# A two-block transformer kernel: the output projection behind the attention loop cut into pieces by its last head, and three changes of order

## What is computed

```python
h = _rmsnorm(hres, norm_g[i, 0])
qkv = jnp.einsum('bld,de->ble', h, w_in)              # 8 heads, q and k of two parts of 64, v of 128
...
a = (p[:, :, 0] - lam * p[:, :, 1]).astype(v.dtype)   # p: softmax of each part with a distance bias
outs.append(jnp.einsum('bhqk,bkhe->bqhe', a, v[:, :qe]))
o = _rmsnorm(o, subln_g) * (1.0 - lam_init)           # per head
return jnp.einsum('ble,ed->bld', o.reshape(bsz, L, N_HEADS * V_DIM), w_out)
...
hres = hres + _rmsnorm(m, norm_g[i, 1])
```

## Time and profile before

| | us |
|---|---|
| median of 3 runs | 2134.41 (2129.05 to 2136.33) |
| the profiled execution, its own time | 2129.2 |
| its span, first to last instruction | 2127.4 |
| TensorE busy, by the page | 1990.0 (94%) |
| VectorE, ScalarE, GpSimd busy | 1056.7, 679.7, 175.9 |
| mean granted TensorE clock | 0.958 of full |

### The profile page before, as it was taken

The page is one execution under the profiler, slowest core; times in us unless marked ns, Lnnn a source line. Parts: engine busy times, 40 slices in busy tenths (PEclk is TensorE's granted clock), DMA queues, the critical chain, the costliest instruction groups (busy, mean ns, idle before and its releaser), DMA issues.

```text
span 2127.4 us, 27654 instructions
## 1 busy us (share of the span) xinstructions
PE 1990.0 (94%) x11486; PEld 1737.7 (82%) x11486; DVE 1056.7 (50%) x1480; ACT 679.7 (32%) x958; POOL 175.9 (8%) x127
## 2 busy tenths in 40 slices
PE   7898888999999988998979999999989989999996
PEld 5677676888888777888869999999989877888885
DVE  7573645543434567565644534333375555343344
ACT  4443433322222335333323413222332233233231
POOL 3000003100000202000003100000210031000002
PEclk9996899999999999999988999999999999999998
DMA  4120102222222321011102122222212222222221
GB/s 168 60 84 35 50 1 79 81 98 99 99 99 79 119 80 60 21 60 41 44 37 80 60 100 100 79 99 81 97 60 100 90 89 79 91 97 89 99 99 40
DMA packets 25907, 166.07 MB, mean 78 GB/s; under 512 B 3792, under 2 KB 4048, under 8 KB 6352
## 3 DMA queue, kind: packets, MB, share of 16 engines
q1 hardware_dynamic: 25808, 164.66, 21.8%
HBM read 162.55 MB, written 2.10 MB: 77 GB/s over the span
## 4 chain that ended last, share of the span: by engine, by line
PE 82%; DVE 11%; issue 4%; ACT 3%; DMA 0%; POOL 0%; SPq 0%; DVEq 0%; ACTq 0%; POOLq 0%
PE ps L306 23%; PE ps L307 23%; PE ps L308 23%; DVE z_lo L413 2%; DVE ps L462 2%; PE ps L1806 2%; DVE w_lo L288 1%; PE ps L1572 1%; DVE h L475 1%; ACT w_hi L277 1%; PE ps L1807 1%; PE ps L1808 1%; PE ps L1574 1%; PE ps L1573 1%; PE ps L1840 1%
## 5 line engine op out<-in xcount | busy, mean ns | idle before, releaser
L306 PE MATMUL ps<-z_hi,w_hi 128*128 128x512 f32 (+1 forms) x1744 | 612.9, 351 | 50.4 <-DVE z_lo L413 34.9
L307 PE MATMUL ps<-z_lo,w_hi 128*128 128x512 f32 (+1 forms) x1744 | 608.3, 349 | 0.0
L308 PE MATMUL ps<-z_hi,w_lo 128*128 128x512 f32 (+1 forms) x1744 | 607.0, 348 | 0.0
L288 DVE TENSOR_TENSOR w_lo<-w_raw,w_hi 128x2048 fp32r<-128x2048 f32 x152 | 348.2, 2291 | 161.6 <-ACT w_hi L277 161.5
L277 ACT ACTIVATE w_hi<-w_raw 128x2048 fp32r<-128x2048 f32 x152 | 289.8, 1906 | 424.3 <-PE ps L308 413.7
L306 PEld LDWEIGHTS ps<-z_hi,w_hi 128*128 128x128 f32 x1744 | 333.9, 191 | 105.0 <-issue 32.7
L306 PE MATMUL ps<-arena,w_hi 128*128 128x256 f32 (+1 forms) x1144 | 385.2, 337 | 5.5 <-DVE arena L1189 5.5
L307 PE MATMUL ps<-arena,w_hi 128*128 128x256 f32 (+1 forms) x1144 | 385.2, 337 | 0.0
L308 PE MATMUL ps<-arena,w_lo 128*128 128x256 f32 (+1 forms) x1144 | 384.6, 336 | 0.0
L308 PEld LDWEIGHTS ps<-z_hi,w_lo 128*128 128x128 f32 x1744 | 333.8, 191 | 44.3
L307 PEld LDWEIGHTS ps<-z_lo,w_hi 128*128 128x128 f32 x1744 | 334.0, 192 | 42.7 <-issue 0.7
(11 more groups left out here) (261 smaller groups left out, 1940.4 us busy)
## 6 DMA issues: line engine op xcount, KB each, us to landing
w_raw<-wstream SPq DMA_DIRECT2D x152, 1024.0 KB, 4.8
h<-xT SPq DMA_DIRECT2D x8, 256.0 KB, 7.1
out<-h SPq DMA_DIRECT2D x8, 256.0 KB, 2.0
rope_cs<-pT SPq DMA_DIRECT2D x1, 512.0 KB, 5.5
acc<-pos SPq DMA_DIRECT2D x1, 256.0 KB, 2.7
acc<-lam SPq DMA_DIRECT2D x1, 128.0 KB, 8.5
sm<-small SPq DMA_DIRECT2D x1, 86.0 KB, 2.5
h<-metaT SPq DMA_DIRECT2D x1, 64.0 KB, 8.8
```

Source lines behind the costliest of these rows:

```text
L288: dve.tensor_tensor(w_lo[:, slot, :], w_raw[:, slot, :], w_hi[:, slot, :].bitcast(f32), ALU.subtract).then_inc(wlo, 1)
L306: pe.matmul(dst, wh, zh, start=(k == 0), stop=False)
L307: pe.matmul(dst, wh, zl, start=False, stop=False)
L308: last = pe.matmul(dst, wl, zh, start=False, stop=(k == nk - 1))
```

## The change

1. The output projection's first six tiles are done in two parts. Part one (input heads 0 to 6, 42 pieces) fills the last head's gaps in the order `EARLY_ORDER`, is copied to `acc` by `out_part1`, and part two (input head 7, 6 pieces) is added by `add_acc_at` from other PSUM banks. Tiles 6 and 7 follow as one block. The weights lie in DRAM in the order of use.
2. The numbers of pieces between a head's steps change: [2] `d_pv(n-1, 1)` [1] `d_v(n)` [2] `d_t(u)` `d_s(u+2)` `o_columns` with [1] and [1] inside, [2] `o_spread` with [1] inside, `d_t(u+1)` `d_s(u+3)` [3] `d_t(u+2)` `d_s_last(u+4, 0)` [3] `d_s_last(u+4, 1)` [2] `d_pv(n, 0)` [1] `d_t(u+3)` [2] `d_s(u+5)` [3] `d_t(u+4)` `d_s(u+6)`. In the last head the three at `d_t(u+2)` are two, the one before `d_t(u+3)` is two, and the three before `d_t(u+4)` are four. Before `d_v(0)` there are three instead of two.
3. VectorE's second weight split of heads 0, 2, 4, 6 moves behind `d_mix(u+3)`.
4. In the first projection VectorE splits block b+1 before it takes the tiles of block b, for b = 3 to 6.

```diff
-MANY = {B_UQ: 4, B_UKV: 4, B_PLEP: 4}
+MANY = {B_UQ: 4, B_UKV: 4, B_PLEP: 4, B_OUT2: 4}
+EARLY = 6
+EARLY_ORDER = [(j, k) for j in range(2) for k in range(6)] + [(0, 6), (1, 6)] + [(j, k) for j in range(2, EARLY) for k in range(7)]
@@ ScalarE, after the loop @@
+            act_hi(act, B_OUT2 % 2, (B_OUT2 + 2) // 2 + 1, 2 * P_OUT2 + 3)
             d_hi(5 * HEADS - 1)
             o_square(HEADS - 1)
+            act_hi(act, (B_OUT2 + 1) % 2, (B_OUT2 + 3) // 2 + 1, 2 * P_OUT2 + 5)
             o_high(HEADS - 1)
...
@@ VectorE, first projection @@
             for j0 in range(0, 8, 2):
+                dve_lo(dve, 4 + j0 // 2, (j0 // 2) % 2)
                 for q in range(2):
                     dve_take(dve, 3 + j0 // 2, q, S, tt(q)[:, 4:4 + S], RX)
-                dve_lo(dve, 4 + j0 // 2, (j0 // 2) % 2)
@@ VectorE, attention loop @@
-                    if m % 2:
-                        w_next(B_QKV + (3 * m + 3) // 2)
...
+                else:
+                    out_part1(0)
+                    out_part1(1)
                 d_min(u + 4, 1)
                 d_mix(u + 3)
+                if m < HEADS and m % 2:
+                    w_next(B_QKV + (3 * m + 3) // 2)
...
+                else:
+                    out_part1(2)
+            w_next(B_OUT2 + 2)
+            out_part1(3)
             d_lo(5 * HEADS - 1)
             d_out(HEADS - 1, 1)
             o_mean(HEADS - 1)
+            out_part1(4)
+            w_next(B_OUT2 + 3)
             o_scale(HEADS - 1)
             o_low(HEADS - 1)
-            out_tiles(B_OUT2, P_OUT2, NLATE)
+            out_part1(5)
+            for k in range(EARLY):
+                add_acc_at(EARLY + k, k, across(2 * (k % 4), NLATE))
+            w_next(B_MLP2)
+            for o in range(2):
+                dve_take(dve, P_OUT2 + 6, o, NLATE, ac(6 + o)[:, LATE:])
@@ TensorE @@
+            def out2_end():
+                pe.wait_ge(s("d_olo"), KD)
+                for tile in range(EARLY):
+                    pe.wait_ge(ps_free, 2 * P_OUT2 + max(EARLY + tile - 3, EARLY))
+                    out2_piece(EARLY * (KD - 1) + tile, across(2 * (tile % 4), NLATE), KD - 1, True, True)
...
@@ TensorE, column sums and spreading @@
+                    if i == 1 or i == 3:
+                        fill(1)
                 last.then_inc(s("d_st"), 1)
...
+                    if i == 2:
+                        fill(1)
                 last.then_inc(s("d_spread"), 1)
@@ TensorE, a head @@
+                more = n + 1 < HEADS
+                fill = qkv if more else out2
+                fill(2)
                 if n:
                     d_pv(n - 1, 1)
-                out2_first(0) if last_head else qkv(2)
+                fill(1)
                 d_v(n)
...
-                out2_first(2) if last_head else qkv(4)
+                fill(3 if more else 2)
                 d_t(u + 2)
@@ TensorE, after the loop @@
-            out2_first(5)
+            out2(3)
             d_pv(HEADS - 1, 1)
-            out2_first(6)
-            o_columns(HEADS - 1)
-            o_spread(HEADS - 1)
-            out2_first(7)
+            out2(3)
+            o_columns(HEADS - 1, out2)
+            out2(2)
+            o_spread(HEADS - 1, out2)
+            out2(EARLY * (KD - 1) - piece)
+            out2_end()
...
-            for j in range(1, 4):
-                gemm(B_OUT2 + j, NLATE, z=late_part, by_tile=(j == 3))
```

More of the change, by code:

```diff
@@ L1813, in late_part, with out2_piece @@
                 return a_out(x, k, LATE)
[L1815 to L1818 removed]
+            def out2_piece(i, dst, k, first, last):
+                b = B_OUT2 + i // 16
+                if i % 16 == 0:
                     pe.wait_ge(wlo, b + 1)
[L1820 to L1832 removed]
+                at = i % 16 * P
+                wh, wl = w_hi[:, b % 2, at:at + P], w_lo[:, b % 2, at:at + P]
+                for a, e in cuts_of(NLATE):
+                    zh, zl = late_part(0, k)[:, a:e], late_part(1, k)[:, a:e]
+                    pe.matmul(dst[:, a:e], wh, zh, start=first, stop=False)
+                    pe.matmul(dst[:, a:e], wh, zl, start=False, stop=False)
+                    done = pe.matmul(dst[:, a:e], wl, zh, start=False, stop=last)
+                if last:
+                    done.then_inc(ps_full, 1)
@@ new lines, in _, with out2 @@
+            piece = 0
+            def out2(count):
+                nonlocal piece
+                for _ in range(count):
+                    tile, k = EARLY_ORDER[piece]
+                    if k == 0:
+                        pe.wait_ge(ps_free, 2 * P_OUT2 + max(tile - 1, 0))
+                    if tile < 2:
+                        pe.wait_ge(s("d_olo"), k + 1)
+                    out2_piece(piece, across(GEMM_BANK + 2 * (tile % 2), NLATE), k, k == 0, k == KD - 2)
+                    piece += 1
@@ L2074, in pack_weights @@
         block(qkv[tau], qkv[tau + 1])
-    columns(w_out_2[0])
+    o2 = w_out_2[0]
+    pieces = [o2[k * P:(k + 1) * P, j * P:(j + 1) * P] for j, k in EARLY_ORDER]
+    pieces += [o2[(KD - 1) * P:, j * P:(j + 1) * P] for j in range(EARLY)]
+    for at in range(0, len(pieces), 2 * KD):
+        block(*pieces[at:at + 2 * KD])
+    block(col(o2, EARLY * P), col(o2, (EARLY + 1) * P))
     def mlp(up, down):
```

71 lines of the change are left out of this document (31 added, 40 removed).

## The result

| | before | after |
|---|---|---|
| first comparison, median of 4 runs each | 2134.8 (2129.05 to 2136.33) | 2082.65 (2079.39 to 2086.82) |
| the profiled execution, its own time | 2129.2 | 2086.82 |
| all runs of this study, median | 2133.5 (73 runs, 2116.8 to 2139.1) | 2085.4 (14 runs, 2077.0 to 2088.7) |
| mean granted clock, profiled execution | 0.958 | 0.968 |

The two profiled executions differ by 42.4 us; the sum in the prediction was 37.4. Of all runs of this study one was far off, a run of e9 with 3855 us; the ratios leave it out.

What follows compares the result with a forecast made beforehand. TensorE bounds the kernel, so time is won only where it waits or runs at lower clock. 13.6 + 16.9 - 1.3 + 9.4 - 1.2 = 37.4 off 2129.2 gives 2091.8; with half of 5.2 added, 2094, range 2085 to 2108.

Steps and rivals of the forecast that it cites:

- first projection: Blocks 4 to 8: with the split first, TensorE's waits shrink to about 0.1 each; 13.6 us gained.
- head 0, with the piece ahead of `d_v(0)`: Head 0, no norm: waits and slow 3 us before `d_v(1)` go, 3.2 less 0.7 for the added piece; 2.5 us.
- head 1: Head 1 of the attention loop: 1.6 us gained.
- heads 2, 4, 6: Even heads: also lose the wait behind the second weight split and the lower clock following it; 3.4 us gained each.
- heads 3, 5: Odd heads: step-by-step changes in waits and pieces bring a head to 33.2 us; 1.3 gained each.
- clock falls left in heads 0 to 6: Heads 0 to 6: clock still falls in one of seven heads where it hurts; costs 1.3 us.
- last head and tail: Last head and tail: 16.8 us of waits and slow time to be had, 7.4 given back; 9.4 gained.
- clock and squares in the last head: Last head: one clock fall with 0.4 chance, possible delay of squares, 0.3 for GpSimd's sums; costs 1.2 us.
- the rivals: Clock falls each head 2103 (0.17); last head trades waits 2102 (0.12); first projection shrinks less 2099 (0.08); 1.2 GHz heads (0.03).
- The loop of VectorE and ScalarE: First projection: their own loop per block takes 11.3 us against 11.2 for TensorE's block; a rival had 12.5 (chance 0.08).
- the sentence on the Trainium skill: Heads: only longer idle gaps lower the clock; by it the sum is some 8 us less (2102); prediction kept the falls.
- changes between kinds of matmul: Last head: eight more changes between kinds of matmul cost 0.8 us, part of the 7.4 given back.

Runs made afterwards that it cites:

- e9: e5 with VectorE's mean of squares ahead of its first weight split and pieces 3, 2, 2, 4, 2; 2087.9 us, ratio 0.9796.
- e3: Kernel before with only the new piece counts and moved second split for heads 0 to 6; 2112.0 us, ratio 0.9906.
- e5: Changed kernel with column sums and spreading in one piece each, pieces behind them; 2077.9 us, ratio 0.9733.
- e6: Changed kernel with VectorE's second weight split back at its old place ahead of the fifth block's minimum; 2091.2 us, ratio 0.9802.
- e14: e5 plus new order of the last head's end, first weight split of each head moved into idle time ahead of v; 2077.9 us, ratio 0.9734.
- e7: Changed kernel without the two pieces ahead of the second product with v, all three behind it; 2092.4 us, ratio 0.9797.
- e13: e14 with the pieces set to 3, 2, 2, 4, 2 as in e9; 2067.9 us, ratio 0.9677 to the kernel before.
- e1: Kernel before, unchanged, run again; 2131.6 us, ratio 0.9992.
- e2: Kernel before with only the first projection's order changed, VectorE splitting the next weight block before taking tiles; 2115.2 us, ratio 0.9922.

## Why the prediction fell short

By its own steps, in us, from the first pair of profiles:

| step | predicted | measured |
|---|---|---|
| first projection | 13.6 | 13.7 |
| head 0, with the piece ahead of `d_v(0)` | 2.5 | 3.0 |
| head 1 | 1.6 | 1.6 |
| heads 2, 4, 6 | 3.4 each | 4.1 each |
| heads 3, 5 | 1.3 each | 1.4 each |
| clock falls left in heads 0 to 6 | -1.3 | 0 |
| last head and tail | 9.4 | 10.95 |
| clock and squares in the last head | -1.2 | 0 |
| sum | 37.4 | 44.4 |

**Right:** what bounds the kernel, all three mechanisms, and nearly every wait: 0.7 at the spreading (about 0.5 said), 0.8 before `d_s(u+3)` (0.5), 1.5 before `d_pv(7, 1)` (1.7), 1.0 at `d_t(37)` (1.1), 0.3 for the bank (0.5), 0.9 for `out_part1(5)` (0.9). Blocks every 11.14 us (11.3 said), heads of 33.1 (33 to 34). None of the rivals came true in the changed kernel. The loop of VectorE and ScalarE did hold 11.3 or less, the last head's waits are 5.7 us together, and no head runs at the lower clock. One sign of being right was missed on the fast side: the last piece of tile 7 came 64.6 us after `d_v(7)`, not 66 to 68.

**The step that failed is the clock.** It entered as a cost in two places, 1.3 for one fall in seven heads and 1.2 for the last head (with a possible delay of the squares and 0.3 for GpSimd's sums), and both came out at nothing: the granted clock is 1.00 in all stretches above, in 28 of 28 heads of four profiles (the changed kernel's three and e3), and the sums behind the last tile wait 0.2 us for the squares after as before. That is 2.5 of the 7.0 us by which the sum was short; 2.1 are in heads 2, 4 and 6, 1.55 in the last head, 0.5 in head 0, as said below, and 0.3 in small differences. The gains by the clock, the slow time behind the second split and in the last head, were rightly in the sum: they are there in the kernel before and gone after.

This also answers to the sentence on the Trainium skill, "TensorE: Matmul & The Clock Gate", section "Why this matters for your kernels". Its rule, only longer idle gaps to be avoided, would have left out the two costs, rightly; but it would have left out the gains as well, and for the kernel before and for e5, e6, e9 and e14 it does not hold, since there the clock falls beside waits of at most 2.4 us (1.5 in heads 0 to 6 of before). Without its clock terms the sum would have been 5.4 us lower (1.5 three times and 3.4 less 1.3 and 1.2), not 8, and further from what was measured.

The prediction's own reading, that the clock falls where small matmuls and a wait stand together with few pieces between, tells where it can fall, not whether it does. In e6 it falls in heads 2 and 4 and not in head 6, in e5 in heads 1 and 3 and not in 2, 4, 5 and 6, with the same order of steps; and in e7 it holds in all heads beside waits of 1.5. That pieces among the sums help, the rest of the order being the same, is shown (0 of 28 heads against 6 of 21); e13 holds the clock without them. What decides in a single head stays open.

**Mis-sized were three terms.** The moved second split was priced at 0.5 us of TensorE in heads 2, 4 and 6 and costs nothing. The slow time behind its old place is worth the 1.5 that the prediction took (e6), but its own parts for these heads, 1.3 + 1.27 + 1.5 - 0.5, make 3.57 and not 3.4; with the split at nothing they make the 4.1 that was measured. This is 2.1 us in three heads. Head 0 gave 3.7 inside and 0.7 less ahead of it, 0.5 more than booked. In the last head the waits came to 5.7 instead of 6.6 (the eight listed make 6.5), and there is no room for 0.8 of changes between kinds of matmul. In the changed kernel's heads matmuls of a stream start 0.12 apart; a piece starts 0.11 behind the last one-column sum, a one-column sum 0.12 behind a piece, so the new changes cost nothing; only at the scores of 64 rows a change costs 0.09 (0.21 from start to start, where the scores have 264 columns). One thing was counted right for a wrong reason: the pieces among the sums were taken to help against the clock; they do, but they cost a wait of 0.76 in each head (e5), more than they save.

**The base.** The sum was set against the profiled run, with half of its distance to the median. Profile to profile 42.4 were measured: 44.4 of changed stretches and 0.8 at the start (e1 starts 0.2 later than before, e6 0.9 earlier, so this is between runs), less 3.1 in the mLSTM stage. With 44.4 in place of 37.4 the prediction's own base would have given 2087, inside its range. Measured are 2085.4 over 14 runs, just inside too, and 2082.65 over the first four: that these four fell below the range is partly chance of the runs drawn. Against the median of all runs of before, 2133.5, the changed stretches give 2089. The 3.7 us from there to 2085.4 may be how often the clock falls in stages that are the same in both kernels, the mLSTM above all; no run shows it. A range with a low end from the fastest of three runs was too narrow for it: the runs of the kernel before spread over 22 us.

## What to carry to other kernels

Before pricing an edit, compare two executions of the same program stretch by stretch: what differs there (here 3 us in one stage, by the clock alone) is not the edit's. A filler between small steps should stand behind the instruction whose follower on another engine is the next thing waited for, not inside it. When an operation of GpSimd hangs in a critical chain, look at which VectorE instruction starts beside it; a long one with two SBUF inputs cancelled here all that an earlier start was to bring (3.15 us for 1.17).

## What the runs showed of the hardware

- GpSimd's power on 128 x 5 numbers: 1.17 us alone, 3.14 to 3.15 when VectorE's subtraction of 128 x 2048 with two SBUF inputs began ahead of it, ending 1.03 us behind that.
- The granted clock differs between executions of the same instructions: the mLSTM stage is identical in all kernels here. From its first column sums to its last it took 37.00 us in e2, 40.23 in the first profile of before and 43.48 in e1, each with 184 matmuls; here those three:

```profile
162.36:199.36 37.00, 36.70 (x184) 31.82 (x185) 15.31 (x31) 13.27 (x28) 0.00 (x0) 0.70 0.00 1
```

```profile
175.05:215.28 40.23, 39.92 (x184) 34.88 (x185) 15.32 (x31) 13.27 (x28) 0.00 (x0) 0.64 0.00 1
```

```profile
175.06:218.54 43.48, 43.18 (x184) 38.14 (x185) 15.31 (x31) 13.26 (x28) 0.00 (x0) 0.59 0.00 1
```

- A wait can cost its own length again by the lower clock behind it, or not: in e6 a wait of 1.4 us was followed by 1.5 us of lost time in heads 2 and 4 (clock 0.95) and by none in head 6 (1.00).
- Changes between kinds of matmul, start to start in the changed kernel's heads: pieces to transposes or one-column sums 0.12 us, as in a stream of pieces; pieces to scores of 64 rows and 264 columns and back 0.21.
